# Six of eight inner chunks of the second feed-forward matrix as seven block products per pair

## The chip, the core and the metric

The kernel runs on one core of one Trainium2 chip. The metric is the device time of one execution in microseconds (us): 1785.33 before, the median of 3 runs (1785.13 to 1788.58). Names: PE is TensorE (matmuls), PEld its weight loads, DVE is VectorE, ACT is ScalarE, POOL is GpSimd, SP is SyncE, which issues the loads from memory.

## The reference, cut to what matters

Three blocks run one after another on 512 tokens of width 1024. The last two end with the same kind of feed-forward layer, and only that is changed:

```python
def _squared_relu_mlp(h, w1, w2):
    return jnp.square(jax.nn.relu(h @ w1)) @ w2
```

`h` is 512x1024, `w1` 1024x4096, `w2` 4096x1024, all float32. The result is normed, scaled and added to the residual.

## The kernel before

**Precision.** A float32 matmul is made of three in the type fp32r: an operand x is split into a high part (x rounded by an ACT copy) and a low part (x minus the high part), and high times high, high times low and low times high are summed.

**Units.** Weights come in units of 128x2048 elements (1 MB): four tiles of 128 rows, 512 columns wide. Unit u goes through five steps, each on another engine: SP loads it into `wraw[u % 2]`, ACT copies it to `whi[u % 2]` (`hi`, L1477), POOL writes `wlo[u % 2] = wraw - whi` (`lo`, L2040), PE uses it in 48 matmuls of 512 columns (4 banks x 4 tiles x 3), and PE's last matmul frees both buffers for unit u + 2. The semaphores are `w_loaded`, `w_hi`, `w_split` and `w_used`. PE starts a unit only when `w_split` says that its low part is there (`unit_wait`).

**The feed-forward layer** (`mlp0` and `mlp1`, 32 units each) walks over 8 chunks of 512 inner columns. "Up" of a chunk (2 units) makes the hidden tiles, 128 inner columns x 512 tokens in each of the four PSUM banks `PDT`. ACT takes the relu into `mh_r` (L1596), DVE squares it (L2721), ACT makes `mh_hi` (L1600), DVE makes `mh_lo` (L2726). "Down" of a chunk (2 units, one for each half of the 1024 output columns) multiplies the hidden tiles by `w2`; its 8 results (128 tokens x 512) leave PSUM by DVE additions to the accumulator `mixm` (L2743). PE's order is up 0, up 1, down 0, up 2, down 1, up 3, ... up 7, down 6, down 7: three rounds of a loop, with the rest written out. Each engine goes through its own list in order and waits on semaphores. PE's matmuls of down stand at L690 to L692, those of up at L701 to L703.

Of the kernel before, what the change touches and what calls it, by code (L numbers as in the profile page):

```python
# [65 lines left out]
IDX_STEPS = 3 * (H1 // 2)  # L66


def phase_table():
# [3 lines left out]
    def rounds(n):  # L73
# [18 lines left out]
    table["end"] = (unit, list(free), list(full), 0)  # L92
    return table
# [15 lines left out]
def build_program(nc, x, c, w_ada, b_ada, norm_in_gain, w_in, conv_w, conv_b, dt_bias, a_log, d_skip,  # L109
# [13 lines left out]


# [179 lines left out]
    SB_AT = {1: (0, 0), 3: (0, 384), 2: (1, 0), 0: (2, 0)}  # L304

# [167 lines left out]
    def _(sp):  # L473
# [21 lines left out]
        def mlp(name, j):  # L495
            u0 = PH[name][0]

            def up(i, d):
                cc = i * 1024 + 512 * d if isinstance(i, int) else sp.snap(i * 1024 + 512 * d)
                return [w1_v[j][:, 4 * h:4 * h + 4, bass.ds(cc, 512)] for h in range(2)]  # L500

            def down(i, d):
                kk = i * 8 + 4 * d if isinstance(i, int) else sp.snap(i * 8 + 4 * d)
                return [w2_v[j][:, bass.ds(kk, 4), 512 * h:512 * h + 512] for h in range(2)]

            def four(i, first, srcs):
                for n, s in enumerate(srcs):
                    unit(i * 8 + (u0 + first + n), (u0 + first + n) % 2, 4, 512, s)

            four(0, 0, up(0, 0))  # L510
            with sp.Fori(0, 3) as i:
                four(i, 2, up(i, 1))
                four(i, 4, down(i, 0))
                four(i, 6, up(i, 2))
                four(i, 8, down(i, 1))
            four(3, 2, up(3, 1))
            four(3, 4, down(3, 0))
            four(3, 6, down(3, 1))
# [105 lines left out]
        sp.wait_ge(S("first_out"), TT)  # L624
# [2222 lines left out]
```

## Time and profile before

| what | value |
|---|---|
| median of 3 runs | 1785.33 us |
| profiled execution, its span from first to last instruction | 1783.5 us |
| PE busy | 1753.9 us, 98% of the span, 8463 matmuls |
| DVE, ACT, POOL busy | 889.5, 775.7, 633.5 us |
| matmuls of the two feed-forward layers | 3072, of them 1536 for down |

The page's busy times are sums over the whole program, which has stages with different limits. The timeline of one stretch shows each instruction's start, its length and what ended the idle time before it. A matmul's length there (0.39 us) is longer than the distance to the next one, since matmuls overlap: the distance is what counts. The trace's own time beside the runs: the runs' median is 1.8 us above the profiled span, which is what lies around the first and last instruction.

### The profile page before, as it was taken

The page shows a single profiled execution, that of the slowest core. Times are in us where ns is not written, and L with a number is a line of the kernel's source. Part 1 is how long each engine was busy: PE and PEld are TensorE (multiplying, and loading weights), DVE is VectorE, ACT ScalarE, POOL GpSimd, SP SyncE. Part 2 cuts the span into 40 slices and gives each one's busy share as a digit, 9 for nine tenths or more (in the row PEclk, how much of TensorE's full clock was granted, in tenths as well). Part 3 has the DMA queues.
Part 4 walks back from the last instruction along what each step waited for, and adds up shares of the span by engine and source line. Part 5 has one row for each costly group of instructions (what it writes and reads, how often), then busy time and mean ns, then how long its engine had stood idle before and what let it go on. Part 6 is the DMA issues. An engine that isn't in the chain of part 4 may idle for free.

```text
span 1783.5 us, 21728 instructions
## 1 busy us (share of the span) xinstructions
PE 1753.9 (98%) x8463; PEld 1403.9 (79%) x8463; DVE 889.5 (50%) x1336; ACT 775.7 (43%) x1292; POOL 633.5 (36%) x255
## 2 busy tenths in 40 slices
PE   7999999999999999999999999999999999999998
PEld 5888777777787767867988888888866898888886
DVE  6512567676875469852633333345366353333334
ACT  4324566556545343363522222237676542222222
POOL 0443232132253333433444444434410444444442
PEclk9999999999999999999999999999999999999999
DMA  8523322222142312302232222222300232222222
GB/s 308 216 92 105 95 66 67 60 72 71 48 141 75 96 63 94 106 24 83 84 106 95 94 94 94 94 94 81 115 26 1 95 115 98 95 94 94 94 94 83
DMA packets 83920, 166.04 MB, mean 93 GB/s; under 512 B 6041, under 2 KB 8222, under 8 KB 83838
## 3 DMA queue, kind: packets, MB, share of 16 engines
q1 hardware_dynamic: 83838, 164.93, 28.1%
q8 instruction: 53, 0.87, 0.2%
q14 instruction: 29, 0.24, 0.0%
HBM read 157.64 MB, written 2.10 MB: 90 GB/s over the span
## 4 chain that ended last, share of the span: by engine, by line
PE 92%; DVE 4%; ACT 1%; issue 1%; POOL 1%; DMA 0%; SPq 0%; DVEq 0%; ACTq 0%; POOLq 0%
PE PDT L690 13%; PE PDT L692 13%; PE PDT L691 13%; PE PDT L701 10%; PE PDT L702 10%; PE PDT L703 10%; PE PM L1041 2%; PE PM L1315 2%; PE PDT L1276 2%; PE PM L1276 1%; PE PM L1008 1%; PE PM L1068 1%; PE PM L1242 1%; POOL wlo L2040 1%; PE PDT L831 1%
## 5 line engine op out<-in xcount | busy, mean ns | idle before, releaser
L2040 POOL TENSOR_TENSOR wlo<-wraw,whi 128x2048 fp32r<-128x2048 f32 (+3 forms) x170 | 590.5, 3485 | 1006.2 <-ACT whi L1477 831.0
L1477 ACT ACTIVATE whi<-wraw 128x2048 fp32r<-128x2048 f32 (+2 forms) x131 | 244.0, 1863 | 523.2 <-PE PDT L692 300.6
L701 PE MATMUL PDT<-hhi,whi 128*128 128x512 f32 x796 | 312.3, 392 | 0.5 <-POOL wlo L2040 0.5
L703 PE MATMUL PDT<-hhi,wlo 128*128 128x512 f32 x796 | 310.1, 390 | 0.0
L702 PE MATMUL PDT<-hlo,whi 128*128 128x512 f32 x796 | 310.1, 390 | 0.0
L690 PE MATMUL PDT<-whi,hhi 128*128 128x512 f32 (+1 forms) x592 | 233.4, 394 | 1.1 <-DVE hlo L2454 0.6
L692 PE MATMUL PDT<-whi,hlo 128*128 128x512 f32 (+1 forms) x592 | 227.9, 385 | 0.0
L691 PE MATMUL PDT<-wlo,hhi 128*128 128x512 f32 (+1 forms) x592 | 227.8, 385 | 0.0
L690 PE MATMUL PDT<-whi,mh_hi 128*128 128x512 f32 x512 | 199.3, 389 | 0.0
L691 PE MATMUL PDT<-wlo,mh_hi 128*128 128x512 f32 x512 | 199.2, 389 | 0.0
L692 PE MATMUL PDT<-whi,mh_lo 128*128 128x512 f32 x512 | 199.2, 389 | 0.0
L2721 DVE TENSOR_TENSOR mh_r<-mh_r 128x512 f32<-128x512 f32 x64 | 94.5, 1495 | 198.5 <-ACT mh_r L1596 198.5
L2743 DVE TENSOR_TENSOR mixm<-PDT,mixm 128x512 f32<-128x512 f32 x112 | 77.5, 692 | 198.8 <-PE PDT L692 198.8
L703 PEld LDWEIGHTS PDT<-hhi,wlo 128*128 128x128 f32 x796 | 149.4, 188 | 31.6
L701 PEld LDWEIGHTS PDT<-hhi,whi 128*128 128x128 f32 x796 | 149.5, 188 | 31.5 <-issue 1.5
L702 PEld LDWEIGHTS PDT<-hlo,whi 128*128 128x128 f32 x796 | 149.5, 188 | 29.6
L690 PEld LDWEIGHTS PDT<-whi,hhi 128*128 128x128 f32 x592 | 111.1, 188 | 36.8 <-issue 15.1
L692 PEld LDWEIGHTS PDT<-whi,hlo 128*128 128x128 f32 x592 | 111.1, 188 | 22.6
L691 PEld LDWEIGHTS PDT<-wlo,hhi 128*128 128x128 f32 x592 | 111.3, 188 | 21.6 <-issue 1.0
L692 PEld LDWEIGHTS PDT<-whi,mh_lo 128*128 128x128 f32 x512 | 96.1, 188 | 20.1
L690 PEld LDWEIGHTS PDT<-whi,mh_hi 128*128 128x128 f32 x512 | 96.1, 188 | 19.9
L691 PEld LDWEIGHTS PDT<-wlo,mh_hi 128*128 128x128 f32 x512 | 96.1, 188 | 19.8
(385 smaller groups left out, 2422.6 us busy)
## 6 DMA issues: line engine op xcount, KB each, us to landing
wraw<-in_mlp_w SPq DMA_DIRECT2D x64, 1024.0 KB, 5.2
wraw<-in_w_in SPq DMA_DIRECT2D x26, 1024.0 KB, 5.1
wraw<-in_even_w_in SPq DMA_DIRECT2D x16, 1024.0 KB, 5.3
w_ada<-in_w_ada SPq DMA_DIRECT2D x11, 1024.0 KB, 12.6
wraw<-in_w_out SPq DMA_DIRECT2D x8, 1024.0 KB, 5.0
swapped<-qk_sb SPq DMA_DIRECT2D x16, 256.0 KB, 7.3
wraw<-in_even_w_out SPq DMA_DIRECT2D x4, 1024.0 KB, 4.9
wraw<-in_odd_w_o SPq DMA_DIRECT2D x4, 1024.0 KB, 5.6
```

The lines of the kernel that those rows point to most:

```text
L690: mm(bank, sth, wh[:, k, c0:c0 + n], start=start and k == 0, stop=False)
L691: mm(bank, sth, wl[:, k, c0:c0 + n], start=False, stop=False)
L692: last = mm(bank, stl, wh[:, k, c0:c0 + n], start=False, stop=stop and k == kn - 1)
L701: mm(bank, sth, hi[:, k0 + k, :], start=start and k == 0, stop=False)
L702: mm(bank, sth, lo[:, k0 + k, :], start=False, stop=False)
L703: last = mm(bank, stl, hi[:, k0 + k, :], start=False, stop=stop and k == 3)
L1041: op = mm(o, ones_or_triangle[:, :], moving, start=False, stop=last and part is sb_lo, skip_group_check=True)
L1276: last = mm(X[:, b, c0:c0 + w], q(t), k(w), start=t != 0, stop=t != 2, skip_group_check=True)
L1477: nc.scalar.activation(whi[base % 2][:, 0:n], wraw[base % 2][:, 0:n], ACT.Copy).then_inc(S("w_hi"), 1)
L2040: part = g.tensor_tensor(wlo[base % 2][:, cols], wraw[base % 2][:, cols], fl(whi[base % 2][:, cols]), ALU.subtract)
L2721: v.tensor_tensor(mh_r[:, b % 2, :], mh_r[:, b % 2, :], mh_r[:, b % 2, :], ALU.mult)\
L2743: v.tensor_tensor(m, PD[b], m, ALU.add).then_inc(S(f"bank_free{b}"), 1)
```

## The change

Inner chunks 0 to 5 are taken in three pairs (p = 0, 1, 2). The down product of a pair is 512 tokens x 1024 inner by 1024 inner x 1024 output. It is seen as 2x2 blocks: A11, A21 the two token halves of the even chunk, A12, A22 of the odd chunk (256 tokens x 512 inner), and 512x512 blocks of `w2`. Eight block products are replaced by seven (Strassen, in the form with shared sums). In the code they are named P1, P5, P6, P2, P7, P3, P4, in this order. Each has its own "unit" number, its own pair of A parts (`part_hi`, `part_lo`) and its own split of weights, and takes 24 matmuls: 2 token tiles x 4 inner tiles x 3. A layer has 41 units instead of 32. PE's order is up 0, up 1, and for each pair: up 2p+2, seven products, up 2p+3; then down 6, down 7 as before.

What stands around the products:

- ACT: relu and now the square too (`hidden`), the high parts of the A blocks and their sums (`plain_parts`, `summed_parts`, 14 copies of 128x512 a pair), and the high part of each product's weights (`paired_hi`).
- DVE: the sums of A blocks and the low parts (`parts`, 22 instructions of 128x512 a pair), four additions of weight blocks in place (`add_raw`, 128x2048), the low part of all seven products' weights (`raw_lo`, 128x2048), and eight additions or subtractions of a result to `mixm` (`gather`, 2 banks, 1024 elements a partition each).
- POOL: the low parts of the first matrix's units and of the last four down units, but none of the products'.
- PSUM: P1, P6, P7 and P4 go to one half of `PM` and accumulate there, P5, P2 and P3 to the other. A product on a half waits (`mlp_sum`) until DVE has gathered what stood there.
- SP: the same 32 loads a layer, into four raw buffers instead of two. The two new ones lie where the normed input `xn` lies, so units 2 and 3 are loaded only when all of the layer's input is transposed (`tr_done`). The loops are written out. Some semaphores are merged (`x_made`, `rms_after`, `xn_turnable`), with the same points of waiting.

`u0` is the layer's first unit; `PAIRED[p]` = d is the offset of a pair's first product, so that d + 7 and d + 8 are the two units of up 2p+3.

```diff
+MLP_UNITS = 41
+CHUNKS = [0, 2, 4, 13, 15, 24, 26, 35]
+PAIRED = [6, 17, 28]
+ROLES = [(2, 3, 0, 1), (1, 3, 0, 2), (2, 3, 0, 1)]
...
-        ("mlp0", 32, ([24] * 4, [24, 23, 24, 1])),
+        ("mlp0", MLP_UNITS, ([12] * 4, [12, 11, 12, 1])),
...
+            for p, d in enumerate(PAIRED):
+                c = 2 * p
+                split(CHUNKS[c + 1])
+                down(u0 + d + P1, c, 0)
+                split(CHUNKS[c + 1] + 1)
+                down((u0 + d, "b"), c, 1)
+                split(CHUNKS[c + 2])
+                down(u0 + d + P3, c + 1, 1)
+                split(CHUNKS[c + 2] + 1)
+                down(u0 + d + P2, c + 1, 0)
+                split(d + P7)
+                up(c + 3, 0)
+                up(c + 3, 1)
+                split(d + P3)
+                if p < 2:
+                    up(c + 4, 0)
+                    split(d + P4)
+                    up(c + 4, 1)
...
+            def products(p):
+                d, base = PAIRED[p], 24 * layer + 8 * p
+                def product(n, side, start, ready):
+                    u = u0 + d + n
+                    banks = [PM[:, 2 * side + t, :] for t in range(2)]
+                    wh, wl = wview(whi[u % 2], 4, 512), wview(wlo[u % 2], 4, 512)
+                    if ready:
+                        pe.wait_ge(S("mlp_sum"), ready)
+                    pe.wait_ge(S("w_hi"), u + 1)
+                    for t in range(2):
+                        for k in range(4):
+                            rows = slice(t * P, t * P + P)
+                            mm(banks[t], part_hi[n][:, k, rows], wh[:, k, :], start=start and k == 0, stop=False,
+                               skip_group_check=True)
+                            mm(banks[t], part_lo[n][:, k, rows], wh[:, k, :], start=False, stop=False,
+                               skip_group_check=True)
+                    unit_wait(u)
+                    for t in range(2):
+                        for k in range(4):
+                            last = mm(banks[t], part_hi[n][:, k, t * P:t * P + P], wl[:, k, :], start=False, stop=k == 3,
+                                      skip_group_check=True)
+                    last.then_inc(S("w_used"), 1)
+                pe.wait_ge(S("part_made"), 6 * layer + 2 * p + 2)
+                product(P1, 0, True, base)
+                product(P5, 1, True, 0)
+                product(P6, 0, False, base + 1)
+                product(P2, 1, True, base + 3)
+                product(P7, 0, False, base + 4)
+                product(P3, 1, True, base + 5)
+                product(P4, 0, False, base + 6)
...
-            with pe.Fori(0, 3) as i:
-                up(2, i * 6 + 1, i)
-                down(0, 4, i * 6 + 2, i, i * 2)
-                up(6, i * 6 + 4, i)
-                down(1, 8, i * 6 + 5, i, i * 2 + 1)
-            up(2, 19, 3)
-            down(0, 4, 20, 3, 6)
+            up(1)
+            for p in range(3):
+                up(2 * p + 2)
+                products(p)
+                up(2 * p + 3)
+            down()
...
+            def raw_hi(o, slot=None, summed=0):
+                u = u0 + o
+                if summed:
+                    act.wait_ge(S("w_summed"), 12 * layer + summed)
+                elif u in RAW:
+                    slot, loaded = RAW[u]
+                    act.wait_ge(S(f"w_loaded{slot}"), loaded)
+                act.wait_ge(S("w_used"), u - 1)
+                nc.scalar.activation(whi[u % 2][:, :], wraw[slot][:, :], ACT.Copy).then_inc(S("w_hi"), 1)
...
+            def hidden(c, b):
+                r = hid_b[b // 2][:, b % 2, :] if c % 2 else hid_a[:, b, :]
+                full_wait(act, name, b, c, u0 + CHUNKS[c] + 1)
+                if c % 2 and c > 1:
+                    act.wait_ge(S("part_made"), 6 * layer + c - 3 + b // 2 + 1)
+                elif c:
+                    act.wait_ge(S("hid_a_read"), 6 * layer + c - 2 + b // 2 + 1)
+                nc.scalar.activation(r, PD[b], ACT.Relu).then_inc(S(f"bank_free{b}"), 1)
+                act.wait_ge(S(f"bank_free{b}"), PH[name][1][b] + c + 1)
+                nc.scalar.activation(r, r, ACT.Square).then_inc(S("hid_made"), 1)
...
+            for p in range(3):
+                o = CHUNKS[2 * p + 1]
+                raw_hi(o + 2)
+                hidden(2 * p + 1, 0)
+                hidden(2 * p + 1, 1)
+                plain_parts(p, 0)
+                hidden(2 * p + 1, 2)
+                summed_parts(p, 0)
+                raw_hi(o + 3)
+                hidden(2 * p + 1, 3)
+                plain_parts(p, 1)
+                summed_parts(p, 1)
+                paired_hi(p, P1)
+                hidden(2 * p + 2, 0)
+                hidden(2 * p + 2, 1)
+                hidden(2 * p + 2, 2)
+                paired_hi(p, P5)
+                hidden(2 * p + 2, 3)
+                for n in (P6, P2, P7, P3, P4):
+                    paired_hi(p, n)
+                raw_hi(PAIRED[p] + 7)
+                raw_hi(PAIRED[p] + 8)
...
-            pool.wait_ge(S("w_split"), u0 + 3)
-            with pool.Fori(0, 3) as i:
-                for u in range(3, 11):
-                    lo(i, u0 + u, 8)
-            for u in range(27, 33):
-                lo(0, u0 + u, 0)
+            for first, end in ((3, 6), (13, 17), (24, 28), (35, 41)):
+                for u in range(u0 + first, u0 + end):
+                    pool.wait_ge(S("w_split"), u)
+                    pool.wait_ge(S("w_hi"), u + 1)
+                    g.tensor_tensor(wlo[u % 2][:, :], wraw[RAW[u][0]][:, :], fl(whi[u % 2][:, :]), ALU.subtract)\
+                        .then_inc(S("w_split"), 1)
+            lo(0, u0 + MLP_UNITS, 0)
...
+            def raw_lo(o, slot=None):
+                u = u0 + o
+                dve.wait_ge(S("w_hi"), u + 1)
+                raw = wraw[RAW[u][0] if slot is None else slot]
+                v.tensor_tensor(wlo[u % 2][:, :], raw[:, :], fl(whi[u % 2][:, :]), ALU.subtract).then_inc(S("w_split"), 1)
+            def add_raw(to, other, loaded):
+                slot, value = RAW[loaded]
+                dve.wait_ge(S(f"w_loaded{slot}"), value)
+                v.tensor_tensor(wraw[to][:, :], wraw[to][:, :], wraw[other][:, :], ALU.add).then_inc(S("w_summed"), 1)
+            def parts(p, g):
+                tiles = slice(2 * g, 2 * g + 2)
+                a11, a21 = hid_a[:, tiles, 0:2 * P], hid_a[:, tiles, 2 * P:SEQ]
+                a12, a22 = hid_b[g][:, :, 0:2 * P], hid_b[g][:, :, 2 * P:SEQ]
+                s1, s2, s3, s4 = [part_sum[n][:, tiles, :] for n in (P5, P6, P7, P3)]
+                sums, highs = 24 * layer + 8 * p + 4 * g, 42 * layer + 14 * p + 7 * g
+                def low(n, whole, high):
+                    dve.wait_ge(S("part_high"), highs + high)
+                    return v.tensor_tensor(part_lo[n][:, tiles, :], whole, fl(part_hi[n][:, tiles, :]), ALU.subtract)
+                dve.wait_ge(S("hid_made"), 32 * layer + 8 * p + 4 + 2 * g + 2)
+                if p:
+                    dve.wait_ge(S("w_used"), u0 + PAIRED[p - 1] + 7)
+                v.tensor_tensor(s1, a22, a21, ALU.subtract).then_inc(S("part_summed"), 1)
+                v.tensor_tensor(s3, a11, a21, ALU.subtract).then_inc(S("part_summed"), 1)
+                dve.wait_ge(S("part_summed"), sums + 1)
+                v.scalar_tensor_tensor(out=s2, in0=s1, scalar=-1.0, in1=a11, op0=ALU.mult, op1=ALU.subtract)\
+                    .then_inc(S("part_summed"), 1)
+                low(P1, a11, 1).then_inc(S("hid_a_read"), 1)
+                dve.wait_ge(S("part_summed"), sums + 3)
+                v.scalar_tensor_tensor(out=s4, in0=s2, scalar=-1.0, in1=a12, op0=ALU.mult, op1=ALU.subtract)\
+                    .then_inc(S("part_summed"), 1)
+                low(P2, a12, 2)
+                low(P4, a22, 3)
+                low(P5, s1, 4)
+                low(P7, s3, 5)
+                low(P6, s2, 6)
+                low(P3, s4, 7).then_inc(S("part_made"), 1)
...
+            def gather(p, n, side, i, h, op, before):
+                m = mixm[:, 2 * i:2 * i + 2, 512 * h:512 * h + 512]
+                dve.wait_ge(S("w_used"), u0 + PAIRED[p] + n + 1)
+                if 8 * p + before > 0:
+                    dve.wait_ge(S("mlp_sum"), 24 * layer + 8 * p + before)
+                v.tensor_tensor(m, m, PM[:, 2 * side:2 * side + 2, :], op).then_inc(S("mlp_sum"), 1)
+            def products(p):
+                a, b, c, d = [(u0 + slot) % 2 if slot < 2 else slot for slot in ROLES[p]]
+                o = PAIRED[p]
+                add_raw(a, c, u0 + o + P3)
+                gather(p, P1, 0, 0, 0, ALU.add, -3)
+                add_raw(b, c, u0 + o + P3)
+                raw_lo(o + P6, a)
+                gather(p, P5, 1, 1, 1, ALU.subtract, -2)
+                gather(p, P5, 1, 0, 1, ALU.subtract, -1)
+                raw_lo(o + P2)
+                add_raw(a, d, u0 + o + P2)
+                gather(p, P6, 0, 0, 1, ALU.subtract, 3)
+                raw_lo(o + P7, b)
+                gather(p, P2, 1, 0, 0, ALU.add, 1)
+                raw_lo(o + P3)
+                gather(p, P7, 0, 1, 1, ALU.subtract, 2)
+                raw_lo(o + P4, a)
+                gather(p, P3, 1, 0, 1, ALU.subtract, 4)
+                gather(p, P4, 0, 1, 0, ALU.add, 0)
...
+            for p in range(3):
+                parts(p, 0)
+                parts(p, 1)
+                dve.wait_ge(S("w_split"), u0 + PAIRED[p] + P1)
+                raw_lo(PAIRED[p] + P1)
+                a, b = [(u0 + slot) % 2 if slot < 2 else slot for slot in ROLES[p][0:2]]
+                add_raw(a, b, (u0 + PAIRED[p], "b"))
+                raw_lo(PAIRED[p] + P5, a)
+                products(p)
```

On DVE, the first pair's products: ahead of them the low part of P1's weights, behind them the next pair's sums. `wlo` from `whi` is a `raw_lo`, `wraw` from two `wraw` an `add_raw`, `mixm` from PM a `gather`. Before, the stretch of a down chunk (with the squares of the next chunk behind it):

```order
L2743 TENSOR_TENSOR mixm_171<-PDT,mixm_171 128x512 x3
L369 ISA
L2743 TENSOR_TENSOR mixm_171<-PDT,mixm_171 128x512 x4
L369 REGISTER_ALU
L2743 TENSOR_TENSOR mixm_171<-PDT,mixm_171 128x512
L2720 REGISTER_ALU
L2721 TENSOR_TENSOR mh_r_170<-mh_r_170 128x512
```

Now, from the low part of P5 to that of P7:

```order
L2881 TENSOR_TENSOR wlo1_55<-wraw2_170,whi1_53 128x2048
L2887 TENSOR_TENSOR wraw2_170<-wraw2_170,wraw0_50 128x2048
L2934 TENSOR_TENSOR mixm_196<-mixm_196,PM 128x2x512
L2887 TENSOR_TENSOR wraw3_171<-wraw3_171,wraw0_50 128x2048
L2881 TENSOR_TENSOR wlo0_54<-wraw2_170,whi0_52 128x2048
L2934 TENSOR_TENSOR mixm_196<-mixm_196,PM 128x2x512 x2
L2881 TENSOR_TENSOR wlo1_55<-wraw1_51,whi1_53 128x2048
L2887 TENSOR_TENSOR wraw2_170<-wraw2_170,wraw1_51 128x2048
L2934 TENSOR_TENSOR mixm_196<-mixm_196,PM 128x2x512
L2881 TENSOR_TENSOR wlo0_54<-wraw3_171,whi0_52 128x2048
```

Eight additions of 512 elements, spread over 21.8 us of matmuls, have become a dense row of wide instructions, six of them 2048 elements long ahead of the third product's gather.

On POOL, from the accumulator's memset to the end of the layer's first rounds, before (one round of the loop):

```order
L2156 MEMSET mixm_171 128x4096
L2158 UNCONDITIONAL_BRANCH
L2158 ISA
L2040 TENSOR_TENSOR wlo0_54<-wraw0_50,whi0_52 128x2048
L2030 REGISTER_ALU
L2040 TENSOR_TENSOR wlo1_55<-wraw1_51,whi1_53 128x2048
L2030 REGISTER_ALU
L2040 TENSOR_TENSOR wlo0_54<-wraw0_50,whi0_52 128x2048
```

and now. The row with x2 holds two units: the last one ahead of the first pair's products (unit 5) and the first behind them (unit 13). The seven products between them POOL doesn't touch:

```order
L2317 MEMSET mixm_196 128x4096
L2322 TENSOR_TENSOR wlo1_55<-wraw3_171,whi1_53 128x2048
L2322 TENSOR_TENSOR wlo0_54<-wraw0_50,whi0_52 128x2048
L2322 TENSOR_TENSOR wlo1_55<-wraw1_51,whi1_53 128x2048 x2
L2322 TENSOR_TENSOR wlo0_54<-wraw3_171,whi0_52 128x2048
```

On PE, the end of the last product (P4) and the start of the up chunk behind it, now. Before, a down chunk's last matmuls stood ahead of it, and the unit ahead had 48 matmuls, not 24:

```order
L963 MATMUL PM<-whi0_52,part_hi6_181 128x512
L965 MATMUL PM<-whi0_52,part_lo6_195 128x512
L970 MATMUL PM<-wlo0_54,part_hi6_181 128x512 x8
L779 MATMUL PDT<-hhi_56,whi1_53 128x512
L780 MATMUL PDT<-hlo_57,whi1_53 128x512
L781 MATMUL PDT<-hhi_56,wlo1_55 128x512
```

In a product the low part of the weights (`wlo`) is used in the last 8 of the 24 matmuls; in an up unit in the third, and PE waits for it ahead of the first.

## Rows read from the trace of the kernel before

**Rows 1.** The page: busy time of each engine, and PE with its clock in 40 slices.
```profile
span 1783.5 us, 21728 instructions
PE 1753.9 (98%) x8463; PEld 1403.9 (79%) x8463; DVE 889.5 (50%) x1336; ACT 775.7 (43%) x1292; POOL 633.5 (36%) x255
PE   7999999999999999999999999999999999999998
PEclk9999999999999999999999999999999999999999
...
PE 92%; DVE 4%; ACT 1%; issue 1%; POOL 1%; DMA 0%; SPq 0%; DVEq 0%; ACTq 0%; POOLq 0%
```

**Rows 2.** Windows: stretches of mlp0: one down unit, two units, nearly the whole layer.
```profile
core 0: us, PE busy (x) PEld busy (x) DVE busy (x) ACT busy (x) POOL busy (x), PEclk, DMA share, GB/s
945.44:956.32 10.88, 10.88 (x49) 9.01 (x48) 4.06 (x6) 3.56 (x4) 4.60 (x1) 1.00 0.15 39
934.56:956.32 21.76, 21.76 (x97) 18.02 (x96) 10.45 (x11) 8.42 (x10) 9.20 (x2) 1.00 0.22 65
878.80:1203.00 324.20, 324.20 (x1438) 268.76 (x1437) 114.95 (x131) 95.76 (x104) 133.53 (x29) 1.00 0.29 97
```

**Rows 3.** Timeline of PE, from one down unit to the next: start, length, instruction.
```profile
955.64 0.39 PE L690 MATMUL PDT<-whi,mh_hi 128*128 128x512 f32 x1
955.87 0.39 PE L691 MATMUL PDT<-wlo,mh_hi 128*128 128x512 f32 x1
956.10 0.39 PE L692 MATMUL PDT<-whi,mh_lo 128*128 128x512 f32 x1
956.32 0.39 PE L690 MATMUL PDT<-whi,mh_hi 128*128 128x512 f32 x1
956.55 0.39 PE L691 MATMUL PDT<-wlo,mh_hi 128*128 128x512 f32 x1
```

**Rows 4.** Timeline of ACT and POOL: the splitting of the unit after next.
```profile
956.58 1.92 ACT L1477 ACTIVATE whi<-wraw 128x2048 fp32r<-128x2048 f32 x1 [7.15 <-PE PDT L692]
...
958.58 4.61 POOL L2040 TENSOR_TENSOR wlo<-wraw,whi 128x2048 fp32r<-128x2048 f32 x1 [4.46 <-ACT whi L1477]
```

**Rows 5.** Timeline of POOL, then of PE: a place where PE waits for POOL.
```profile
74.09 4.95 POOL L2040 TENSOR_TENSOR wlo<-wraw,whi 128x2048 fp32r<-128x2048 f32 x1 [10.41 <-ACT whi L1477]
...
79.19 0.50 PE L701 MATMUL PDT<-hhi,whi 128*128 128x512 f32 x1 [0.54 <-POOL wlo L2040]
79.52 0.39 PE L702 MATMUL PDT<-hlo,whi 128*128 128x512 f32 x1
79.75 0.39 PE L703 MATMUL PDT<-hhi,wlo 128*128 128x512 f32 x1
```

**Rows 6.** Single lines of the kernel on DVE: 128x2048 in SBUF, and 128x512; min/median/max ns.
```profile
L2746 DVE TENSOR_TENSOR wlo<-wraw,whi x2: 2292/2292/2293, 876.6 to 1445.9; 128x2048 fp32r<-128x2048 f32 x2
L2721 DVE TENSOR_TENSOR mh_r<-mh_r x64: 676/693/4721, 878.8 to 1733.2; 128x512 f32<-128x512 f32 x64
L2726 DVE TENSOR_TENSOR mh_lo<-mh_r,mh_hi x64: 677/690/695, 880.2 to 1734.6; 128x512 fp32r<-128x512 f32 x64
```

**Rows 7.** Timeline of DVE at the end of mlp0: 512 elements from PSUM, 1024 from SBUF.
```profile
1199.62 0.69 DVE L2767 TENSOR_TENSOR mixm<-PDT,mixm 128x512 f32<-128x512 f32 x1
1200.40 1.23 DVE L2776 TENSOR_TENSOR mixr<-mixm,row_a 128x1024 f32<-128x1024 f32 x1
1201.55 1.28 DVE L2200 SCALAR_TENSOR_TENSOR xn<-xres,rstd,row_c 128x1024 f32<-128x1024 f32 x1
```

**Rows 8.** Timeline of POOL and of DVE: squares and additions beside a POOL pass.
```profile
936.82 4.60 POOL L2040 TENSOR_TENSOR wlo<-wraw,whi 128x2048 fp32r<-128x2048 f32 x1 [6.29 <-ACT whi L1477]
949.51 4.60 POOL L2040 TENSOR_TENSOR wlo<-wraw,whi 128x2048 fp32r<-128x2048 f32 x1 [8.10 <-ACT whi L1477]
...
938.17 4.40 DVE L2721 TENSOR_TENSOR mh_r<-mh_r 128x512 f32<-128x512 f32 x2 [13.60 <-ACT mh_r L1596]
942.67 0.69 DVE L2726 TENSOR_TENSOR mh_lo<-mh_r,mh_hi 128x512 fp32r<-128x512 f32 x1
951.08 0.69 DVE L2743 TENSOR_TENSOR mixm<-PDT,mixm 128x512 f32<-128x512 f32 x1 [2.03 <-PE PDT L692]
```

**Rows 9.** Timeline of ACT: relu and the copy to the high part.
```profile
943.46 0.60 ACT L1596 ACTIVATE mh_r<-PDT 128x512 f32<-128x512 f32 x1 [0.82 <-DVE mh_lo L2726]
943.95 0.62 ACT L1600 ACTIVATE mh_hi<-mh_r 128x512 fp32r<-128x512 f32 x1
```

**Rows 10.** The page: loads of the feed-forward weights: count, KB each, us to landing.
```profile
wraw<-in_mlp_w SPq DMA_DIRECT2D x64, 1024.0 KB, 5.2
```

**Rows 11.** Timeline of PE and ACT, start of mlp0: the last transposes, and unit 2's high part.
```profile
865.84 1.03 PE L748 MATMUL PM<-ident,xn 128*128 128x128 f32 x8
...
874.64 1.92 ACT L1477 ACTIVATE whi<-wraw 128x2048 fp32r<-128x2048 f32 x1 [7.08 <-PE PDT L836]
```

More of the change, by code:

```diff
@@ L92, in phase_table, with raw_table, load @@
     table["end"] = (unit, list(free), list(full), 0)
+    return table
+def raw_table(PH):
+    count, table = [0] * 4, {}
+    def load(key, slot):
+        count[slot] += 1
+        table[key] = (slot, 16 * count[slot])
+    for name, (u0, _, _, units) in PH.items():
+        if name in ("mlp0", "mlp1"):
+            for *key, slot in MLP_LOADS:
+                slot = (u0 + slot) % 2 if slot < 2 else slot
+                load(u0 + key[0] if len(key) == 1 else (u0 + key[1], "b"), slot)
+        else:
+            for u in range(u0, u0 + units):
+                load(u, u % 2)
     return table
@@ L304, in build_program @@
     SB_AT = {1: (0, 0), 3: (0, 384), 2: (1, 0), 0: (2, 0)}
+    P1, P5, P6, P2, P7, P3, P4 = range(7)
     QB_AT = {3: (0, 0), 2: (1, 0), 0: (1, 384), 1: (2, 0)}
@@ L493, in columns, with mlp, into, up @@
             loop(sp, n_chunks, body)
-        def mlp(name, j):
+        def mlp(name, j, tiles):
             u0 = PH[name][0]
[L498 to L518, printed above, removed]
+            def into(key, src):
+                slot = RAW[key][0]
+                sp.dma_start(wview(wraw[slot], 4, 512), src).then_inc(S(f"w_loaded{slot}"), 16)
+            def up(c, h):
+                into(u0 + CHUNKS[c] + h, w1_v[j][:, 4 * h:4 * h + 4, 512 * c:512 * c + 512])
+            def down(key, c, h):
+                into(key, w2_v[j][:, 4 * c:4 * c + 4, 512 * h:512 * h + 512])
+            def split(offset):
+                sp.wait_ge(S("w_split"), u0 + offset + 1)
+            split(-2)
+            up(0, 0)
+            split(-1)
+            up(0, 1)
+            sp.wait_ge(S("tr_done"), TR[tiles][0] + 8)
+            up(1, 0)
+            up(1, 1)
+            split(0)
+            up(2, 0)
+            split(1)
+            up(2, 1)
+            for p, d in enumerate(PAIRED):
[16 more added lines that the diff above has]
+                    up(c + 4, 1)
+            down(u0 + 37, 6, 0)
+            split(PAIRED[2] + P4)
+            down(u0 + 38, 6, 1)
+            split(36)
+            down(u0 + 39, 7, 0)
+            split(38)
+            down(u0 + 40, 7, 1)
@@ L1634, in mlp_sums @@
+            for b in range(4):
+                plain_high(layer, 6, b)
+            raw_hi(37)
+            for b in range(4):
+                if b == 3:
+                    raw_hi(38)
+                hidden(7, b)
+                plain_high(layer, 7, b)
+            raw_hi(39)
+            raw_hi(40)
         def mlp_sums(name):
@@ L2758, in last_sum @@
+            for b in range(4):
+                plain_low(7, b)
+            dve.wait_ge(S("mlp_sum"), 24 * layer + 24)
+            for h in range(2):
+                for b in range(4):
+                    full_wait(dve, name, b, 8 + h, u0 + 37 + h)
+                    m = mixm[:, b, 512 * h:512 * h + 512]
+                    v.tensor_tensor(m, PD[b], m, ALU.add).then_inc(S(f"bank_free{b}"), 1)
         def last_sum(name, h):
```

221 lines of the change are left out of this document (100 added, 121 removed), and 3 rows, old and new, of the table MLP_LOADS.

## The prediction

> **What bounds the kernel now.** I read the page first. PE is busy 98% of the span, and the chain that ended last is PE for 92% of it; the granted clock is in its top tenth in every slice, the upper of the two levels, 2.4 GHz [rows 1]. Then the windows of mlp0: over 324.20 us PE is busy 324.20 us [rows 2], so the feed-forward layer has no idle time at all, while POOL works 133.53, DVE 114.95 and ACT 95.76 us of it. Only fewer matmuls, or cheaper ones, can shorten this stage, and whatever is added elsewhere costs nothing as long as it comes in time. The timeline of PE gives the price of a matmul: starts at 955.64, 955.87, 956.10, 956.32, 956.55 [rows 3]. Over a whole unit it is 10.88 us for 48 matmuls [rows 2, 3], 226.7 ns each. (The length of 0.39 us overlaps the next one and isn't the price.)
>
> **What is removed.** A pair's down products were 4 units x 48 = 192 matmuls; seven products x 24 are 168. With 24 fewer, three pairs, two layers, 144 matmuls go, all from a stage where PE never waits: 144 x 0.2267 = 32.6 us. The remaining ones keep their form (128x128 stationary, 512 moving columns), so I keep their price.
>
> The Trainium skill, page "TensorE: Matmul & The Clock Gate", section "Back-to-back issue gap", gives about 131 ns as the sustained distance of matmuls of 512 columns with weight loads. The trace disagrees, since every distance here is 226.7 ns. By that figure, as an estimate, the saving would be 144 x 0.131 = 18.9 us and the time 1785.3 - 18.9 + 10.1 = 1776.5 us; with every distance in that group against it, it gets no chance of its own.
>
> **The new wait: the unit behind the products.** A unit's low part is ready a fixed time after the unit two places ahead is used up. The steps: the last matmul of that unit is issued, the next unit's first one starts at 956.32, and ACT starts the high part at 956.58, 0.26 later. POOL starts at 958.58, 2.00 later, and takes 4.61 [rows 3, 4]. So the low part is there 0.26 + 2.00 + 4.61 = 6.87 us after the first matmul of the unit in between. Before, that unit lasted 10.88 us, with 4.0 to spare. Now the unit ahead of up 2p+3 is product P4, which lasts 24 x 0.2267 = 5.44 us. An up unit waits for its low part ahead of its first matmul. Where PE waits for POOL in the trace, POOL ends at 74.09 + 4.95 = 79.04 and the matmul starts at 79.19, 0.15 later; the next comes 0.33 later instead of 0.23, another 0.10 [rows 5]. The wait is 6.87 + 0.15 + 0.10 - 5.44 = 1.68 us, once for each pair: 6 x 1.68 = 10.1 us. With POOL at 4.95, as in the other row, it is 2.02 each and 12.1 in all. The product P4's low part, on which POOL also waits, isn't later: ACT makes its high part 0.26 to 2.18 us into P3, DVE takes 2.29, so it is there 4.5 us into P3. The second unit of up 2p+3 has a whole unit of 10.88 us ahead of it and isn't late. The unit's load: SP issues it when P7's low part is ready, about 22.6 us after P1's start (below), and the high part is wanted at 6 x 5.44 + 0.26 = 32.9. A load takes 5.2 us [rows 10], and two in a row no more than 10.4: it lands at 33.0 at the latest, at 27.8 if alone. Nothing to add.
>
> **What DVE must do inside the products.** This is the part on which the change stands or falls, so I follow the queue. Time 0 is P1's first matmul; products start at 0, 5.44, 10.88, 16.32, 21.76, 27.2, 32.64, and the up chunk is due at 38.1. DVE's price for 2048 elements from SBUF is 2.29 us [rows 6], in a dense row 2.21 (the next starts 0.08 before an instruction's end, as 1200.40 + 1.23 to 1201.55 shows [rows 7]). A gather reads 1024 elements from PSUM. The trace has 512 from PSUM at 0.69, the same as 512 from SBUF, and 1024 from SBUF at 1.23 [rows 6, 7]; I take 1.23, in a row 1.15. The bounds are 2 x 0.69 = 1.38 above and 1.23 below. ACT's high part of P5 needs the last up unit used up: 0.26 to 2.18. DVE then: low of P5 to 4.5; addition for P6 to 6.7; gather P1 (done at 5.7) to 7.8; addition for P7 to 10.0; low of P6 to 12.3 (ACT's high of P6 came at about 8.7); two gathers of P5 (done at 11.1) to 14.6; low of P2 to 16.8; addition for P4 to 19.0; gather P6 to 20.2; low of P7 to 22.4; gather P2 to 23.6; high of P3 is there at 23.9, its low at 26.2; gather P7 at 27.5 to 28.7; low of P4 at 29.4 to 31.7; gathers of P3 and P4 as they end. The dates of PE: P6 may start once P1 is gathered (7.8 against 10.88), P2 once P5 is (14.6 against 16.32, 1.7 to spare), P7 once P6 is (20.2 against 21.76, 1.6 to spare). Low parts are needed 16 matmuls, 3.6 us, into a product, and each is 2 to 4 us early. So DVE's work of 8 x 2.29 + 8 x 1.23 = 28.2 us in 38.1 us hides. It is the densest place: six wide instructions and four gathers stand between P5's high part and P6's gather, 17.9 us of work in 19.5 us of time. With gathers at 1.38 it is 18.5, which still fits.
>
> **What DVE and ACT must do ahead of the products.** Before, two squares that begin under a POOL pass take 4.40 us instead of 1.3: POOL runs from 936.82 to 941.42 and the squares end at 942.57. An addition with one operand in PSUM, at 951.08 under a POOL pass of 949.51 to 954.11, takes its 0.69 [rows 8]. So DVE instructions with two operands in SBUF stand still until POOL's pass is over, and gathers don't. That is what the Trainium skill says in "SBUF — State Buffer", section "Who interferes with whom": a DVE instruction with two SBUF inputs and a GpSimd one that reads SBUF exclude each other, and who comes first keeps the port for its whole instruction. It speaks against the change, which puts 22 such DVE instructions a pair beside POOL's passes; by it, these passes have to be added in full, as follows. The second half of a pair's sums starts behind POOL's pass over the last up unit. That unit's high part waits for ACT's copies of the first half and ends at about -18.5 (ACT has then had relu and square of three banks and seven copies at 0.6 each [rows 9]), the pass lasts until -13.8. The 11 instructions of 128x512 (0.69, in a row 0.61 [rows 6]) end at -6.9, the low part of P1 and the addition for P5 (2 x 2.21) at -2.5. They are due at 0.26, so 2.8 us are to spare. P1's low part itself is due at 3.6. POOL never passes between P1 and P4, save the pass for the unit behind, which meets only gathers.
>
> **Costs that I set at zero.** ACT's squares (DVE's before): ACT has 95.76 us of work in 324.20 [rows 2] and is ahead of every date above. Written-out loops: mlp0's last chunks are written out already, and the window that holds them and the loops has no idle time [rows 2]. Units 2 and 3 loaded after the last transposes: these end at 866.87, a load lands 5.2 later at 872.1, and unit 2's high part isn't started before 874.64 anyway [rows 10, 11]. Two loads in a row would be at 877.3, and unit 3's high part isn't wanted before about 880.
>
> **The sum.** Against the profiled execution: 1783.5 - 32.6 + 10.1 = 1761.0 us of span. The median of the runs lies 1.8 above the span, so 1762.8 us for a run, 1.3% less.
>
> **Rivals.** *DVE late inside the products.* For: the spare time is 1.6 us on 17.9 us of work, and gathers of two banks and additions in place have no row of their own. Against: in-place squares cost the same as other instructions (693 ns against 690 [rows 6]). If the ten instructions take 10 to 20% more, 1.8 to 3.6, the third gather is 0.2 to 2.0 us late in each pair, 1 to 12 us in all: 1764 to 1775 us. *DVE's queue becomes the bound: slower than before.* The place is the same: if a 4.6 us POOL pass fell into the chain ahead of P6's gather, P7 would be 4.6 - 1.6 = 3.0 late in each pair, 18 us in all, 1781 us; two passes, or 9.2, make 7.6 late, 45.6 in all, 1808 us. It is slower from 1.6 + 22.5 / 6 = 5.4 us of additional DVE time in each pair. Against: POOL's order has no pass there. *The wait behind the products doesn't appear* (PE begins the unit with what it has, or the pass of POOL is shorter next to an idle DVE): the saving is whole, 1785.3 - 32.6 = 1752.7 us. Against: the wait stands ahead of the first matmul, and 29 passes in mlp0 have a mean of 4.6. *Nothing is saved*, as when a product costs PE what 1.14 products did (a restart of PSUM accumulation or a wait that breaks PE's row at each product): 24 x 6 x 0.2267 is 32.6 us, or 0.78 us at each of 42 products; with the 1.68 waits, 0.54 at each is enough. It ends at about 1785. Against: PE passes 8 bank changes and their waits in each down chunk without a gap [rows 2].
>
> **How the numbers follow.** Forecast, 1758 to 1768 us: 0.66. DVE late, 1768 to 1780: 0.14. Wait absent or nearly, below 1758: 0.09. Nothing saved, within 0.2% of before (3.6 us, about what a measurement of this kernel can tell from no change): 0.04. Slower: 0.07. So faster 0.89, same 0.04, slower 0.07. The range that holds 8 in 10 takes in the forecast with POOL at 4.95 and the lower part of the late DVE: 1756 to 1773 us.
>
> **What would show it.** Right: in each pair PE idles once, 1.6 to 2.1 us, ahead of the first matmul of up 2p+3, released by POOL; 42 products of 5.44 us each follow one another without a gap; DVE's additions and low parts of 2048 elements take 2.29 and gathers 1.2; no matmul waits for DVE. Wrong: a wait of PE for a gather (`mixm`) ahead of P2 or P7, or for a DVE low part; a POOL pass starting between P1 and P3; a DVE pass of over 2.5 us inside the products; matmul distances above 0.23 us.

## Result and the profile after

The changed kernel takes 1762.82 us (median of 4 runs, 1762.65 to 1764.26) against 1785.95 us before (4 runs, 1785.13 to 1788.58). The ratio is 0.9871, with a 95% interval from 0.9857 to 0.9885. The forecast was 1762.8 us, with a range from 1756 to 1773.

The page of the changed kernel, as in [rows 1]: span, busy time of each engine, the clock in 40 slices, shares of the chain that ended last.

```profile
span 1760.7 us, 21220 instructions
PE 1723.1 (98%) x8319; PEld 1376.0 (78%) x8319; DVE 1019.2 (58%) x1374; ACT 868.7 (49%) x1410; POOL 523.1 (30%) x231
...
PEclk9999999999999999999999999999999999999999
...
PE 89%; DVE 4%; POOL 3%; ACT 2%; issue 2%; DMA 0%; SPq 0%; ACTq 0%; POOLq 0%; DVEq 0%
```

PE has 8463 - 8319 = 144 matmuls less. POOL's share of the chain has risen from 1% to 3%: something of the critical path now goes through it. DVE has 130 us more work, ACT 93, POOL 110 less, and none of this shows in the time by itself.

Who ended PE's waits, over the whole program (line waited at, releaser, us in total, times, longest):

```profile
PE PDT L779 <- POOL wlo L2322: 8.2, 6, 1.4
PE PDT L1037 <- DVE xn L2436: 5.2, 3, 4.4
PE PM L826 <- DVE xn L2362: 4.1, 4, 1.8
```

The first row is new, six times 1.4 us, once for each pair. The other two stand before the change too, outside the feed-forward layers. No row has a product (L963, L965, L970) waiting for DVE.

Three windows of mlp0 (columns as in [rows 2]): the first six products of the first pair, the last product P4 with what follows it, and most of the layer.

```profile
923.42:956.06 32.64, 32.64 (x145) 27.03 (x144) 26.96 (x15) 12.63 (x8) 0.00 (x0) 1.00 0.27 97
956.06:963.03 6.97, 5.61 (x26) 4.32 (x24) 2.44 (x2) 3.19 (x2) 4.59 (x1) 1.00 0.48 151
880.00:1190.00 310.00, 305.92 (x1348) 252.28 (x1347) 178.56 (x148) 138.60 (x155) 78.35 (x17) 1.00 0.28 95
```

Six products take 32.64 us, 5.44 each, with PE busy throughout. DVE is busy 26.96 of these 32.64 us, 83%. P4 with the wait behind it takes 6.97 us. In the long window 4.1 us of idle PE stand where before there was none [rows 2]: three times 1.36.

A distance that leaves out the rest of the program is that from the first matmul of one pair's P1 to that of the next pair's. A pair has 168 matmuls of products and 192 of up chunks, and 360 x 0.2267 is 81.60 us. Here the distance is 83.26 and 83.27 us in mlp0 (P1 starts at 923.42, 1006.68 and 1089.95). Each pair thus costs 1.67 us beside its matmuls.

### The profile page after: what moved, and what is told of

It reads as the page before. It is cut to its first block, busy times and chain, and to the rows that moved or that the text cites. A ratio compares the mean times of both kernels' runs of the same rounds, so it can differ in the third digit from the quotient of the medians.

```text
span 1760.7 us, 21220 instructions
## 1 busy us (share of the span) xinstructions
PE 1723.1 (98%) x8319; PEld 1376.0 (78%) x8319; DVE 1019.2 (58%) x1374; ACT 868.7 (49%) x1410; POOL 523.1 (30%) x231
## 4 chain that ended last, share of the span: by engine, by line
PE 89%; DVE 4%; POOL 3%; ACT 2%; issue 2%; DMA 0%; SPq 0%; ACTq 0%; POOLq 0%; DVEq 0%
PE PDT L779 10%; PE PDT L781 10%; PE PDT L780 10%; PE PDT L768 9%; PE PDT L770 8%; PE PDT L769 8%; PE PM L970 4%; PE PM L963 4%; PE PM L965 4%; PE PM L1153 2%; PE PM L1427 2%; POOL wlo L2322 2%; PE PDT L1388 2%; PE PM L1388 2%; PE PM L1120 1%
## 5 line engine op out<-in xcount | busy, mean ns | idle before, releaser
L2201 POOL TENSOR_TENSOR wlo<-wraw,whi 128x512 fp32r<-128x512 f32 (+5 forms) x112 | 323.4, 2905 | 629.3 <-ACT whi L1589 454.4
L2322 POOL TENSOR_TENSOR wlo<-wraw,whi 128x2048 fp32r<-128x2048 f32 x34 | 156.7, 4609 | 464.4 <-ACT whi L1705 464.4
L1705 ACT ACTIVATE whi<-wraw 128x2048 fp32r<-128x2048 f32 x78 | 149.5, 1916 | 274.0 <-PE PM L970 120.5
L1589 ACT ACTIVATE whi<-wraw 128x2048 fp32r<-128x2048 f32 (+3 forms) x71 | 129.2, 1820 | 174.5 <-PE PDT L770 75.8
L2881 DVE TENSOR_TENSOR wlo<-wraw,whi 128x2048 fp32r<-128x2048 f32 x44 | 100.6, 2287 | 55.0 <-ACT whi L1705 55.0
L963 PE MATMUL PM<-whi,part_hi 128*128 128x512 f32 x336 | 130.7, 389 | 0.0
L965 PE MATMUL PM<-whi,part_lo 128*128 128x512 f32 x336 | 130.7, 389 | 0.0
L770 PEld LDWEIGHTS PDT<-whi,hlo 128*128 128x128 f32 x592 | 111.1, 188 | 22.5
L2905 DVE TENSOR_TENSOR part_sum<-hid_b,hid_a 128x512 f32<-128x512 f32 x12 | 29.3, 2439 | 119.4 <-ACT hid_b L1729 119.4
L970 PE MATMUL PM<-wlo,part_hi 128*128 128x512 f32 x336 | 83.0, 389 | 0.0
L2934 DVE TENSOR_TENSOR mixm<-mixm,PM 128x1024 f32<-128x1024 f32 x48 | 57.8, 1215 | 38.9 <-PE PM L970 38.9
```

The lines of the kernel that those rows point to most:

```text
L770: last = mm(bank, stl, wh[:, k, c0:c0 + n], start=False, stop=stop and k == kn - 1)
L963: mm(banks[t], part_hi[n][:, k, rows], wh[:, k, :], start=start and k == 0, stop=False, skip_group_check=True)
L965: mm(banks[t], part_lo[n][:, k, rows], wh[:, k, :], start=False, stop=False, skip_group_check=True)
L970: last = mm(banks[t], part_hi[n][:, k, t * P:t * P + P], wl[:, k, :], start=False, stop=k == 3, skip_group_check=True)
L1705: nc.scalar.activation(whi[u % 2][:, :], wraw[slot][:, :], ACT.Copy).then_inc(S("w_hi"), 1)
L2201: part = g.tensor_tensor(wlo[base % 2][:, cols], wraw[base % 2][:, cols], fl(whi[base % 2][:, cols]), ALU.subtract)
```

## The experiments

All are edits of the changed kernel. Where a span is named, it is that of the profiled execution; the changed kernel's is 1760.7 us.

**The wait taken away by DVE.** DVE makes the low part of the first up unit behind the products.

```diff
                 gather(p, P3, 1, 0, 1, ALU.subtract, 4)
+                raw_lo(o + 7)
                 gather(p, P4, 0, 1, 0, ALU.add, 0)
...
-            for first, end in ((3, 6), (13, 17), (24, 28), (35, 41)):
+            for first, end in ((3, 6), (14, 17), (25, 28), (36, 41)):
```

> Undoes the one wait: the low part of the first up unit behind the products is made by DVE (2.29 us) instead of POOL (4.6 us), between the gathers of P3 and P4; all else as in the changed kernel. My theory (the gap of 1.63 us in each pair is POOL's pass arriving late): high part 0.26 to 2.18 us into P4, low part by DVE there at about 4.5, before PE's date of 5.44, so the gap goes and the time falls by 6 x 1.63 = 9.8 us, from 1762.8 to about 1753.0. Rival A (turning from the products to an up chunk costs PE a gap by itself): the gap stays, 1762.8. Rival B (DVE has no room at this place, the gather of P4 or the next sums come late): the gap goes, but another wait of PE for DVE appears, 1755 or more.

Measured: 1753.86 us (4 runs, 1753.46 to 1754.14), ratio 0.9822 (0.9806 to 0.9838), span 1751.5. Expected were 1753.0. The timeline of its DVE around P4, which here starts at 956.87:

```profile
957.07 1.22 DVE L2934 TENSOR_TENSOR mixm<-mixm,PM 128x1024 f32<-128x1024 f32 x1 [1.14 <-PE PM L970]
959.08 2.29 DVE L2881 TENSOR_TENSOR wlo<-wraw,whi 128x2048 fp32r<-128x2048 f32 x1 [0.79 <-ACT whi L1705]
962.51 1.22 DVE L2934 TENSOR_TENSOR mixm<-mixm,PM 128x1024 f32<-128x1024 f32 x1 [1.14 <-PE PM L970]
```

The low part is there at 961.37, 4.50 us into P4, and PE goes on at 962.31 without a gap. It fits into a hole between two gathers. The distance of two P1 is 81.60 us (1005.83 to 1087.43), which is the 360 matmuls and nothing else. So 1.67 us went in each pair, 10.0 in all; the span fell by 9.2 because in this execution the first product starts 0.81 us later (924.23 against 923.42), ahead of everything that the edit touches. So neither the turn from products to an up chunk costs PE anything, nor was DVE short of room here.

**The same wait taken away on PE's side.** POOL keeps its pass, but the first unit of up 2p+3 takes its matmuls with low weights last.

```diff
...
+                pe.wait_ge(S("w_hi"), u + 1)
+                for b in range(4):
+                    bank_wait(name, b, c)
+                    for k in range(4):
+                        st = wh[:, k, b * P:b * P + P]
+                        mm(PD[b], st, hhi[:, k, :], start=k == 0, stop=False, skip_group_check=True)
+                        mm(PD[b], st, hlo[:, k, :], start=False, stop=False, skip_group_check=True)
+                unit_wait(u)
+                for b in range(4):
+                    for k in range(4):
+                        last = mm(PD[b], wl[:, k, b * P:b * P + P], hhi[:, k, :], start=False, stop=False,
+                                  skip_group_check=True)
+                last.then_inc(S("w_used"), 1)
...
-                up(2 * p + 3)
+                up_low_last(2 * p + 3)
```

> Removes the same wait in another way: POOL keeps its pass, but the first unit of up 2p+3 starts with its 32 matmuls of high weights and takes the 16 of low weights last; so PE needs the low part only 7.25 us into the unit, 12.7 us after P4's start, and POOL has it at 6.9. My theory: again 6 x 1.63 = 9.8 us less, about 1753.0, with POOL's pass where it was. Rival A (the turn itself costs): 1762.8. Rival B (matmuls in another order over four banks cost more than 226.7 ns): between 1753 and 1763, seen in the distances.

Measured: 1753.36 us (4 runs, 1752.4 to 1753.91), ratio 0.9817 (0.98 to 0.9833), span 1751.7. Its POOL, and its PE at the turn:

```profile
959.44 4.62 POOL L2348 TENSOR_TENSOR wlo<-wraw,whi 128x2048 fp32r<-128x2048 f32 x1 [47.78 <-ACT whi L1731]
...
962.56 0.39 PE L956 MATMUL PDT<-hhi,whi 128*128 128x512 f32 x1
962.78 0.39 PE L957 MATMUL PDT<-hlo,whi 128*128 128x512 f32 x1
```

POOL's pass runs to 964.06, 1.5 us past PE's start of the unit, and costs nothing now. The distance of two P1 is 81.60 us here too (the first product starts at 924.48, 1.06 later than in the changed kernel's execution). Both ways give back the same, 9.0 and 9.5 us of the median and 9.2 and 9.0 of the span. These two are faster than the changed kernel and the one before; between themselves they can't be told apart.

**Filling the gap.** n matmuls between P4 and up 2p+3, whose result is overwritten.

```diff
                 products(p)
+                bank_wait(name, 0, 2 * p + 3)
+                for _ in range(n):
+                    mm(PD[0], hhi[:, 0, 0:P], hhi[:, 0, :], start=True, stop=True, skip_group_check=True)
                 up(2 * p + 3)
```

With n = 7:

> Seven matmuls of 512 columns more between P4 and up 2p+3 in each pair (7 x 0.2267 = 1.59 us of PE work; their result is overwritten). My theory (PE waits for a date that POOL sets): they fit into the 1.63 us of waiting, so the time stays at 1762.8, within 0.5 us. Rival (the gap is a cost of PE's own, or follows PE's last product): 6 x 1.59 = 9.5 us more, 1772.3.

Measured: 1763.46 us (4 runs, 1762.17 to 1765.3), span 1760.6 against 1760.7. The timeline of PE:

```profile
961.29 1.75 PE L1021 MATMUL PDT<-hhi 128*128 128x512 f32 x7
962.87 0.47 PE L779 MATMUL PDT<-hhi,whi 128*128 128x512 f32 x1
963.18 0.40 PE L780 MATMUL PDT<-hlo,whi 128*128 128x512 f32 x1
```

Forty-two matmuls more for nothing. POOL's pass ends at 962.79 in this execution, the seven matmuls from 961.29 on fill PE's row to 962.88, and the up chunk starts at 962.87. The distance of two P1 is 83.27 to 83.29 us, against 83.26 and 83.27 without them. The median is 0.64 us above the changed kernel's, a little more than the 0.5 expected; with runs that spread over 3 us this says nothing against the distance. With n = 24:

> Twenty-four matmuls more in each pair (results overwritten), so that PE has the 192 matmuls a pair that it had before the change, with everything else of the change left in. My theory: 5.44 us more less the 1.63 of waiting that they fill, 6 x 3.81 = 22.9 us, 1785.7, the time of the kernel before; the whole gain is the matmuls. Rival (part of the gain is something else, such as written-out loops, squares on ACT or loads into four buffers): a time clearly below 1785, or above it, where these cost.

Measured: 1786.54 us (10 runs, 1785.23 to 1787.05) against 1785.53 before on the same chip, ratio 1.0002 (0.9993 to 1.0012), span 1784.7. The distance of two P1 is 87.03 to 87.05 us, and 384 matmuls are 87.04: 3.77 us more in each pair, 22.6 in all, which with the changed kernel's span makes 1783.3. The other 1.4 us lie ahead of the feed-forward layer, in code that the edit doesn't touch: the first product starts at 924.80 in this execution and at 923.42 in that of the changed kernel. The window of the layer has no idle PE:

```profile
880.00:1190.00 310.00, 310.00 (x1374) 256.98 (x1374) 172.43 (x140) 136.40 (x148) 75.64 (x17) 1.00 0.27 93
```

So with PE's matmuls put back, the kernel is as fast as the one before. Squares on ACT, written-out loops, four raw buffers and 130 us more on DVE together cost nothing that can be measured. The run tests them together, not one by one.

**DVE's room inside the products.** One, and then two, additional passes of 2048 elements ahead of P2's low part.

```diff
+            def again(o):
+                u = u0 + o
+                dve.wait_ge(S("w_hi"), u + 1)
+                link(v.tensor_tensor(wlo[u % 2][:, :], wraw[RAW[u][0]][:, :], fl(whi[u % 2][:, :]), ALU.subtract))
...
+                for _ in range(n):
+                    again(o + P2)
                 raw_lo(o + P2)
                 add_raw(a, d, u0 + o + P2)
```

One:

> Adds one DVE pass of 128x2048 in each pair's products: the low part of P2's weights is written twice, the second time behind the first (about 2.3 to 2.4 us more of DVE, the result is the same). My theory (DVE's chain up to P6's gather has 1.7 us to spare: it ends 20.0 us into the products, P7 is due at 21.76): P7 starts 0.6 to 0.8 us late in each pair, 4 to 5 us in all, about 1767.5. Rival A (DVE is the bound already, hidden somewhere): the whole pass shows, 6 x 2.3 = 14 us, 1776.8. Rival B (PE doesn't depend on this chain): 1762.8.

Measured: 1768.5 us (4 runs, 1767.44 to 1768.64), ratio 0.9901 (0.9884 to 0.9917), span 1765.3, which is 4.6 above 1760.7. Its DVE and then its PE around the start of P7:

```profile
944.41 1.21 DVE L2939 TENSOR_TENSOR mixm<-mixm,PM 128x1024 f32<-128x1024 f32 x1
...
945.68 0.50 PE L963 MATMUL PM<-whi,part_hi 128*128 128x512 f32 x1 [0.50 <-DVE mixm L2939]
946.01 0.39 PE L965 MATMUL PM<-whi,part_lo 128*128 128x512 f32 x1
```

P6's gather ends at 945.62, P7 starts 0.06 later; it was due at 945.02. With the slow second matmul each pair loses 0.66 + 0.11 = 0.77 us; the distance of two P1 grows by 0.80, 4.8 in all. Of a pass of 2.3 us, 0.8 show. The median is 5.7 above the changed kernel's, beyond the 4 to 5 expected: the profiled execution is the fastest of the four, and the others' spans lie 1.0 to 1.2 above its own. Two:

> As the one with one additional DVE pass, but two (about 4.7 us more of DVE in each pair). My theory: P2's low part comes at 21.3 us instead of 19.95, 1.4 to 1.5 late, and P7 then waits for P6's gather another 1.5: 3.0 to 3.2 us in each pair, 18 to 19 us in all, about 1781.5: each microsecond beyond the spare 1.7 shows in full. Rival A (the queue falls further and further behind, later products are late as well): more than 28 us, above 1791, slower than the kernel before. Rival B (no dependence): 1762.8.

Measured: 1781.8 us (8 runs, 1781.32 to 1784.54), ratio 0.9976 (0.9965 to 0.9987), span 1782.4. The profiled execution is the slowest of the eight. Who ended PE's waits:

```profile
PE PDT L779 <- POOL wlo L2322: 8.2, 6, 1.4
PE PM L970 <- DVE wlo L2881: 7.8, 6, 1.3
PE PM L963 <- DVE mixm L2939: 7.3, 6, 1.2
```

As expected, first P2's low part and then P6's gather are late. P2's matmuls with low weights start at 946.27, 1.46 us after they are due, and P7 at 949.61, 2.99 late. The distance of two P1 is 86.38 to 86.39 us, 3.1 more, and it doesn't grow from pair to pair: the delay of one isn't handed on to the next. That is 18.7 us in six pairs; the other 3.0 by which this slowest execution's span exceeds the changed kernel's lie outside of the pairs, 1.4 of them ahead of the first product. With two passes some four fifths of the change's gain are gone.

**One low part given back to POOL.** It is that of P6's weights; DVE waits for it ahead of its own low part of P2's.

```diff
-                raw_lo(o + P6, a)
...
+                dve.wait_ge(S("w_split"), u0 + o + P2)
                 raw_lo(o + P2)
...
-            for first, end in ((3, 6), (13, 17), (24, 28), (35, 41)):
+            for first, end in ((3, 6), (8, 9), (13, 17), (19, 20), (24, 28), (30, 31), (35, 41)):
...
+                    if u - u0 in (8, 19, 30):
+                        slot = ROLES[(u - u0 - 8) // 11][0]
+                        slot = (u0 + slot) % 2 if slot < 2 else slot
...
```

> Moves one part back to POOL: the low part of P6's weights. POOL's pass of 4.6 us may start when ACT's high part is there, 8.7 us into the products; at this time DVE is in an addition of two SBUF blocks (7.75 to 10.04). My theory (the two exclude each other): POOL gets through from about 10.0 to 14.65, PE wants it at 14.5 and is 0.3 to 0.5 us late in each pair, 2 to 3 us in all, about 1765; DVE's low part of P2 starts when POOL ends. Rival (they don't exclude each other for additions in place): POOL's pass runs 8.7 to 13.4, nothing is late, 1762.8, and DVE's next two-operand pass starts within it.

Measured: 1763.39 us (4 runs, 1762.98 to 1764.18), span 1761.7, 1.0 above that of the changed kernel. Its POOL, then DVE, ACT having delivered the high part at 931.87:

```profile
932.01 5.72 POOL L2327 TENSOR_TENSOR wlo<-wraw,whi 128x2048 fp32r<-128x2048 f32 x1 [21.63 <-ACT whi L1705]
...
930.96 2.29 DVE L2892 TENSOR_TENSOR wraw<-wraw,wraw 128x2048 f32<-128x2048 f32 x1
934.29 2.35 DVE L2939 TENSOR_TENSOR mixm<-mixm,PM 128x1024 f32<-128x1024 f32 x2 [1.04 <-PE PM L970]
937.76 2.29 DVE L2886 TENSOR_TENSOR wlo<-wraw,whi 128x2048 fp32r<-128x2048 f32 x1 [1.12 <-POOL wlo L2327]
```

POOL's row begins at 932.01, while DVE's addition runs until 933.25, and it lasts 5.72 us instead of 4.6. From the addition's end it is 4.48. So POOL stood still behind the addition in place, and the gathers of P5 at 934.29 ran under POOL at their full pace. The place and the direction are as expected, the size is smaller: PE's matmuls with P6's low weights start 0.07 us late, at 937.79, and the distance of two P1 is 83.45 to 83.51 us, 0.2 more than in the changed kernel: 1.2 in all (1.0 by the spans), where 2 to 3 were expected. The 1763.39 can't be told from 1762.82 by the medians alone; the trace shows the delay.

## Why the prediction was right

**The saving.** 144 matmuls at 226.7 ns, 32.6 us. The products keep this price: six of them take 32.64 us, and a pair without its wait takes 360 times 226.7 ns. Putting 144 matmuls back gives the old time, which is the direct test. By the Trainium skill's figure of 131 ns ("TensorE: Matmul & The Clock Gate", section "Back-to-back issue gap") the saving would have been, as an estimate, 18.9 us; the changed kernel's trace, with 226.7 ns, disagrees with it as that of the kernel before did. The recorded 1776.5 us for that case isn't a whole sum: its 10.1 us of waiting were worked out with 226.7 ns, and with shorter matmuls P4 would be shorter and the wait longer.

**The new wait.** The forecast was 1.68 us for each pair. PE at the turn, and POOL's pass:

```profile
963.03 0.50 PE L779 MATMUL PDT<-hhi,whi 128*128 128x512 f32 x1 [1.36 <-POOL wlo L2322]
963.36 0.40 PE L780 MATMUL PDT<-hlo,whi 128*128 128x512 f32 x1
...
958.38 4.59 POOL L2322 TENSOR_TENSOR wlo<-wraw,whi 128x2048 fp32r<-128x2048 f32 x1 [47.78 <-ACT whi L1705]
```

P4 starts at 956.06, its 24 matmuls would end it at 961.50, the next one comes at 963.03: 1.53, and 0.10 more for the slow second matmul, 1.63. The full loss is 1.67, by the distance of two P1 (83.27 - 81.60) and by its 81.60 in the two runs without the wait; the 0.04 between the two are small delays of the next few matmuls. Single steps were off and made up for each other. The step from POOL's end to PE's start, taken as 0.15 from [rows 5], is 0.06 here (962.97 to 963.03); POOL starts 2.06 us after ACT instead of 2.00 and takes 4.59 instead of 4.61; and what PE loses on going on is 0.14 in all instead of 0.10. So PE's idle time alone, 1.53, is just below the 1.6 to 2.1 that were to show the forecast right, and the whole loss is within. The wait view's 1.36 is shorter than the loss, since it counts from the modelled end of the last matmul; the distance of starts is the number to use. Two ways of removing the wait gave back 9.0 to 9.5 us of the median and 10.0 in the pairs, and seven matmuls put into it cost nothing, so its cause is shown, not only argued.

**DVE's queue.** The hand-made list of dates held. DVE from P1's start at 923.42:

```profile
925.63 2.29 DVE L2881 TENSOR_TENSOR wlo<-wraw,whi 128x2048 fp32r<-128x2048 f32 x1 [4.06 <-ACT whi L1705]
927.84 2.28 DVE L2887 TENSOR_TENSOR wraw<-wraw,wraw 128x2048 f32<-128x2048 f32 x1
930.04 1.21 DVE L2934 TENSOR_TENSOR mixm<-mixm,PM 128x1024 f32<-128x1024 f32 x1
931.17 2.29 DVE L2887 TENSOR_TENSOR wraw<-wraw,wraw 128x2048 f32<-128x2048 f32 x1
933.38 2.29 DVE L2881 TENSOR_TENSOR wlo<-wraw,whi 128x2048 fp32r<-128x2048 f32 x1
...
942.25 1.21 DVE L2934 TENSOR_TENSOR mixm<-mixm,PM 128x1024 f32<-128x1024 f32 x1
```

P6's gather ends 943.46 - 923.42 = 20.04 us into the products; the forecast was 20.2, and P7 is due at 21.76. The two prices that had no row, an addition in place and a gather of two banks, came out at 2.28 and 1.21 (taken: 2.29 and 1.23). DVE works without a pause from 925.63 until that gather's end. The spare time of 1.6 us was 1.7, and the additional passes showed that it is real and that it is all there is. The rival of a late DVE was thus right in mechanism, with a price of 0.8 us a pair for 2.3 us of work; it just didn't occur.

**The sums ahead of the products.** DVE's first sum of the second half starts under POOL's pass, as foreseen:

```profile
906.71 4.44 DVE L2905 TENSOR_TENSOR part_sum<-hid_b,hid_a 128x512 f32<-128x512 f32 x1 [2.02 <-ACT hid_b L1729]
...
905.99 4.62 POOL L2322 TENSOR_TENSOR wlo<-wraw,whi 128x2048 fp32r<-128x2048 f32 x1 [8.27 <-ACT whi L1705]
```

It takes 4.44 us instead of 0.69 and ends half a microsecond after POOL. One date was off: in the first pair the pass starts 17.4 us ahead of P1, not 18.4 (in the other two of mlp0 18.85). In the first pair ACT's relu of the third bank waits 0.99 us for DVE to have read the other chunk, a wait in the code (`hid_a_read`) that I had passed over. DVE's addition for P5 ends at 921.58, 1.8 us ahead of P1 instead of 2.5, so it took 0.7 of the 2.8 us to spare, and nothing of the time.

**Costs set at zero** were zero taken together, by the run with 24 filling matmuls: its ratio's interval is -0.07 to +0.12%, and its pairs take 87.04 us, their 384 matmuls.

The mechanism and the terms held: 22.6 us less in six pairs by the distances of P1 (a pair's 384 matmuls took 87.04, it now takes 83.27), where 32.6 - 10.1 = 22.5 were forecast. That the time came out within 0.1 us is luck all the same. The executions differ by 1 to 3 us. The profiled span is 1760.7 us, 0.3 below the forecast's 1761.0, and the run lies 2.1 above its span where 1.8 was taken; the two cancel. And the forecast started from 1785.33 us, while with one run more the median before is 1785.95: the measured fall is 23.1 us, 0.6 more than forecast.

## What to carry to other kernels

When a change makes a unit of PE's work shorter, look for what was hidden behind its old length: here a chain of three engines, 6.9 us long and started when the unit two places ahead is used up, fitted behind 10.9 us and not behind 5.4, and cost a third of the gain. It is found with one subtraction, and taken away by giving that one step to the engine with a hole at that place, or by ordering the matmuls so that the late operand is used last. To see whether an engine that is busy 83% of a stretch is near to being the bound, write its instructions with their dates against the dates at which each is wanted; the busy share tells neither the 1.7 us to spare nor that the next microsecond shows in full.

## What the runs showed that I had not expected

POOL's pass behind a DVE instruction with two SBUF operands shows as a longer row (5.72 us, of which 1.24 are waiting), which starts 0.14 us after ACT's high part is there; DVE's row under POOL does the same (4.44 us for 0.69). In these two cases a long row wasn't slow work, so what ran on the other engine until its end has to be looked up. And after a wait PE loses 0.10 to 0.11 us more between its first and second matmul (0.33 to 0.34 instead of 0.23), seen behind POOL and behind a gather. Behind a low part made by DVE, in the run with two additional passes, three matmuls take 0.96 us together, where without a wait ahead of them they take 0.84.
